# Both softmax attentions one step deeper: values of a head behind turns and scores of the next ones, two buffers of turned copies

## The reference, cut to what matters

```python
# MLA, 8 heads, per block of 128 queries
sc = jnp.einsum('bqhd,bkhd->bhqk', q[:, s:e], k[:, :e]).astype(jnp.float32)
sc = jnp.where(mask[None, None], sc, MASK_VALUE)
p = jax.nn.softmax(sc, axis=-1).astype(v.dtype)
outs.append(jnp.einsum('bhqk,bkhd->bqhd', p, v[:, :e]))
```

## Time and profile before

| | before |
|---|---|
| median of 3 runs | 1555.76 us (1552.83 to 1557.51) |
| profiled execution | 1555.55 us |
| its span | 1553.7 us |
| PE busy | 1458.6 us, 94% |
| DVE busy | 766.3 us, 49% |
| ACT busy | 617.6 us, 40% |
| mean granted clock of PE | 0.942 of full |
| MLA attention | 591 to 661 us of the span |
| MoBA attention | 1135 to 1174 us of the span |

### The profile page before, as it was taken

One profiled execution on the slowest core, in us unless ns is written; L12 is line 12 of the kernel. 1 busy time (PEld: TensorE's weight loads), 2 busy tenths in 40 slices (PEclk: granted clock), 3 DMA queues, 4 the chain that ended last, 5 costly groups with the idle time before them and its releaser, 6 DMA issues.

```text
span 1553.7 us, 26186 instructions
## 1 busy us (share of the span) xinstructions
PE 1458.6 (94%) x10140; PEld 1239.5 (80%) x10140; DVE 766.3 (49%) x1288; ACT 617.6 (40%) x1014; POOL 10.5 (1%) x23
## 2 busy tenths in 40 slices
PE   5999999999998998899999989999878899999996
PEld 4899999899997995489999889799747855555553
DVE  4466654656546663356665456865166431222123
ACT  4445553443434552344444356533143422232222
POOL 0000020000000000000000000000000000000000
PEclk8999999999999997799999989999658899999998
DMA  7654445655555442456555444432003349999992
GB/s 309 127 186 136 136 163 176 231 174 172 173 175 217 161 152 95 155 188 227 190 185 184 161 176 150 138 109 99 23 0 109 109 170 374 370 354 370 370 367 97
DMA packets 80139, 289.65 MB, mean 186 GB/s; under 512 B 9520, under 2 KB 10544, under 8 KB 79920
## 3 DMA queue, kind: packets, MB, share of 16 engines
q1 hardware_dynamic: 77760, 280.00, 50.0%
q0 software_dynamic: 1712, 3.68, 1.5%
q10 hardware_dynamic: 576, 4.65, 0.7%
HBM read 285.14 MB, written 3.15 MB: 186 GB/s over the span
## 4 chain that ended last, share of the span: by engine, by line
PE 84%; DVE 8%; ACT 3%; issue 2%; DMA 2%; SPq 0%; ACTq 0%; DVEq 0%
PE bank L652 17%; PE bank L656 16%; PE bank L655 16%; PE bank L1178 11%; PE bank L1146 4%; DMA ring<-weights 2%; PE bank L716 2%; PE bank L793 2%; PE bank L687 1%; ACT w_hi L1249 1%; PE bank L1168 1%; PE bank L1169 1%; DVE ring_low L1631 1%; DVE sq L1969 1%; PE bank L1008 1%
## 5 line engine op out<-in xcount | busy, mean ns | idle before, releaser
L1631 DVE TENSOR_TENSOR ring_low<-ring,w_hi 128x1024 fp32r<-128x1024 f32 x292 | 356.0, 1224 | 314.5 <-ACT w_hi L1249 311.9
L652 PE MATMUL bank<-hn_hi,w_hi 128*128 128x272 f32 (+1 forms) x1456 | 426.4, 293 | 22.4 <-DVE ring_low L1631 8.6
L656 PE MATMUL bank<-hn_hi,ring_low 128*128 128x272 f32 (+1 forms) x1456 | 419.3, 288 | 0.0
L655 PE MATMUL bank<-hn_low,w_hi 128*128 128x272 f32 (+1 forms) x1456 | 418.7, 288 | 0.0
L1249 ACT ACTIVATE w_hi<-ring 128x1024 fp32r<-128x1024 f32 x292 | 307.3, 1055 | 225.9 <-PE bank L652 181.0
L652 PEld LDWEIGHTS bank<-hn_hi,w_hi 128*128 128x128 f32 x1456 | 278.5, 191 | 29.2 <-DVE hn_low L1650 13.2
L656 PEld LDWEIGHTS bank<-hn_hi,ring_low 128*128 128x128 f32 x1456 | 279.1, 192 | 0.0
L655 PEld LDWEIGHTS bank<-hn_low,w_hi 128*128 128x128 f32 x1456 | 278.7, 191 | 0.2
L652 PE MATMUL bank<-arena_r,w_hi 128*128 128x256 f32 (+1 forms) x848 | 245.4, 289 | 12.0 <-DVE mod L1679 2.9
L656 PE MATMUL bank<-arena_r,ring_low 128*128 128x256 f32 (+1 forms) x848 | 242.9, 286 | 0.0
L655 PE MATMUL bank<-arena_r,w_hi 128*128 128x256 f32 (+1 forms) x848 | 242.4, 286 | 0.0
(11 more groups left out here) (333 smaller groups left out, 1444.1 us busy)
## 6 DMA issues: line engine op xcount, KB each, us to landing
ring<-weights SPq DMA_DIRECT2D x532, 512.0 KB, 4.2
tab<-tables ACTq DMA_DIRECT2D x1, 3129.0 KB, 12.7
skew<-arena POOLq DMA_DIRECT2D x1, 2048.0 KB, 46.5
h<-tokens ACTq DMA_DIRECT2D x2, 544.0 KB, 4.1
tab<-skew POOLq DMA_DIRECT2D x8, 128.0 KB, 3.6
out<-hn SPq DMA_DIRECT2D x8, 128.0 KB, 2.0
tab<-skew POOLq DMA_DIRECT2D x8, 64.0 KB, 3.4
vec<-vectors ACTq DMA_DIRECT2D x1, 321.5 KB, 4.9
```

What stands on the lines that cost most here:

```text
L652: begun = mm(dst[:, 0:cols], wh, high(k), start=k == 0, stop=False)
L655: mm(dst[:, 0:cols], wh, low(k), start=False, stop=False)
L656: last = mm(dst[:, 0:cols], wl, high(k), start=False, stop=k == K - 1)
L1631: tt_(ring_lo[:, slot, :], ring[:, slot, :], w_hi[:, n % SPLITS, :], ALU.subtract).then_inc(S("w_lo_ready"), 1)
```

## The change

The turned buffers pt_m, pt_meta and pt_a get two parts each, by j % 2. For that up_t, which follows pt_a in the arena, moves to a place that is free by then. On TensorE the loop has one round more: round j does T(j), S(j + 2) and then V(j - 1), with M or J of head j - 1 in front. On ACT, store moves from head i - 1 to head i - 2, and ACT makes the meta copy in MLA, which DVE made. On DVE, the function of head i - 1 becomes that of head i - 2, and the last one stands behind the loop. In MLA this function has lost the meta copy and still does low of the head before its own. In MoBA it now does low of its own head, so that low(j) is done in the same round as before and the norm piece one round later.

```diff
-        pt_m = carve(1, 3 * P)
-        pt_meta = carve(1, SEQ)
+        pt_m = carve(2, 3 * P)
+        pt_meta = carve(2, SEQ)
...
-        pt_a = carve(1, 3 * P, at=delta_at + 4 * NP * P)
-        up_t = carve(2, SEQ)
+        pt_a = carve(2, 3 * P, at=delta_at + 4 * NP * P)
+        up_t = carve(2, SEQ, at=2 * DT * SEQ)
...
-            def attention(tag, heads, score, put):
+            def attention(tag, heads, score, turn, put):
...
-                for j in range(heads):
-                    pe.wait_ge(S(tag + "_p"), j + 1)
+                for j in range(heads + 1):
+                    if j < heads:
+                        pe.wait_ge(S(tag + "_p"), j + 1)
+                        if j:
+                            pe.wait_ge(S(tag + "_pt"), j)
+                        turn(j)
+                    scores(j + 2)
                     if j:
-                        pe.wait_ge(S(tag + "_pt"), j)
-                    put(j, lambda: scores(j + 2))
+                        put(j - 1)
...
-            def attention(tag, heads, probs, parts, stat, pt, store):
-                for i in range(heads + 1):
+            def attention(tag, heads, probs, parts, stat, pt, store, ptm=None):
+                for i in range(heads + 2):
...
-                    if i >= 1:
+                    if 1 <= i <= heads:
                         j = i - 1
                         act.wait_ge(S(tag + "_turned"), j + 1)
-                        fn(pt[:, 0, :], bank[6][:, 0:3 * P], ACT.Copy).then_inc(S(tag + "_pt"), 1)
-                        store(j)
+                        fn(pt[:, j % 2, :], bank[6][:, 0:3 * P], ACT.Copy).then_inc(S(tag + "_pt"), 1)
+                        if ptm is not None:
+                            act.wait_ge(S(tag + "_turnedm"), j + 1)
+                            fn(ptm[0:META, j % 2, :], bank[7][0:META, 0:SEQ], ACT.Copy).then_inc(S(tag + "_ptm"), 1)
+                    if i >= 2:
+                        store(i - 2)
...
                         last.then_inc(S(tag + "_p"), 1)
-                        if turned:
-                            turned(j)
+                    if turned and i >= 2:
+                        turned(i - 2)
+                if turned:
+                    turned(heads - 1)
...
             def mla_turned(j):
-                dve.wait_ge(S("mla_turnedm"), j + 1)
-                if j:
-                    dve.wait_ge(tile_done, done(am(j - 1)))
-                nc.vector.tensor_copy(pt_meta[0:META, 0, :], bank[7][0:META, 0:SEQ]).then_inc(S("mla_ptm"), 1)
...
-                if j:
-                    o_a_low(j - 1)
+                o_a_low(j)
...
-            o_a_low(AH - 1)
```

## The result

The changed kernel takes 1568.88 us, the median of five runs (1567.63 to 1571.33), against 1555.76 us before. The ratio is 1.0086, 95% interval 1.0064 to 1.0109. The profiled execution took 1571.33 us, the slowest of the five, with a span of 1569.5 us.

A forecast was written before the change was run, and what follows sets the result against it. MoBA was taken as bound by its loop over scores, DVE's front and p, and the turn, 4.63 us a head. 1555.6 + 13.8 (MoBA) + 3.2 (MLA) = 1572.6, stated as 1572.5; range 1565 to 1577.5, own range 1570.5 to 1574.5.

The forecast's parts named there:

- The loop S, front, p, T: MoBA head: scores, DVE's scale and mask, exponentials times reciprocal sum, turned probabilities; said to set the pace, 4.63 us.
- DVE's low as the new link: MoBA: DVE's subtraction of rounded values waits for the moved values step, delaying the next front; 7.04 us a head against 4.63.
- The tail: MoBA's end, from the turn of head 6 to the last values: 7.9 us against 6.13, +1.8.
- MLA's wait of T(1): MLA: the turn of head 1 directly follows the scores of head 2, so TensorE stands still: +2.3 us.
- the term of 2.2: MLA: turn of head 1 and scores of head 3 come before mod sum 4, at half clock: +2.2 us.
- T(7)'s wait of 1.3: MLA's end: no front follows join 6, so the last turn is ready within the values of head 5: -1.3 us.
- MLA's sum: The whole MLA stage: 2.3 + 2.2 - 1.3 = +3.2 us.
- the clock at the end: MLA's end: last turn, last mod sum and values of head 6 stay at half clock; at full, MLA would be +0.6.
- rival 1: MLA's end: last turn and last mod sum run at full clock, total 1570 us; chance 0.15.
- Rival 2: MLA: clock falls already around join 6, so it and values of head 5 run at half, 2.4 us more, 1575; chance 0.10.
- Rival 3: MLA: one more group of turn, scores and values at half clock, total 1577 to 1579 us; chance 0.06.

The follow-up runs named there:

- run 4: Changed kernel with MoBA's low one head later and scores issued ahead of turns in both attentions, two buffers: 1533.8 us, ratio 0.9856.
- run 8: Changed kernel with MoBA's low one head later and scores issued ahead of turns in MoBA alone: 1549.52 us, ratio 0.9964.
- run 1: Changed kernel with only MoBA's low on DVE put back to one head later: 1553.1 us, ratio 0.9981.
- run 2: Kernel before the change, with only MoBA's low on DVE made that of its own head: 1568.53 us, ratio 1.0079.
- run 6: Changed kernel with scores issued ahead of turns in both attentions, MoBA's low kept at its own head: 1541.58 us, ratio 0.9911.
- run 3: Changed kernel with MoBA's order put back to that of the kernel before, leaving the change in MLA alone: 1554.73 us, ratio 1.0003.
- run 5: Kernel before the change, single buffers kept, with scores issued ahead of turns: 1546.46 us, ratio 0.9935.
- run 7: run 4 with the output layer's first three weight units split one mod sum later inside MLA: 1526.76 us, ratio 0.983.

## Why the prediction was right

**What bounds MoBA: right.** The loop S, front, p, T of 4.63 us was read from rows of one head. Cutting it (runs 4, 8) brought the head to TensorE's and DVE's own work, 3.1 to 4.2 us.

**DVE's low as the new link: right, in place and in size.** Sum over the links: 7.04 us a head. Measured: 7.01, 7.15, 7.14, 7.15, 7.01. T(6) to T(7) was 3.96 for 4.1. The tail as a whole is the weaker part: 7.2 us for 7.9, with V(5) ending 2.2 us after T(6) for 2.5, while the five heads grew by 12.3 for 12.0. So MoBA grew by 13.4 us for 13.8. Run 1 removes the link and the loss, run 2 makes the link alone and the loss, run 6 shortens the way to V and the head shrinks as summed. The signs named ahead for MoBA all came: five T's at 7.0 to 7.15 us behind 3.0 idle us, low waiting 2.97 for ACT, front following at once, clock 0.50.

**MLA's wait of T(1): right.** 2.23 us measured for 2.3; T(1) and S(3) ran at half until M4 (4.9 us, 605.30 to 610.22), as the term of 2.2 had it; T(7)'s wait of 1.3 went.

**MLA's sum: mis-sized.** The term that failed is the clock at the end. I took M7, T(7) and V(6) to be at half as before, +3.2 in all, and held rival 1, +0.6, at 0.15. The stage was to be longer by about 3 us, and it is longer by 0.4 in the changed kernel's profile. In the four traces with MLA as changed (changed kernel, runs 1, 3, 8) MLA takes 69.9, 70.7, 68.3 and 70.3 us, mean 69.8. With MLA as before (before, run 2) it takes 69.5 and 68.6, mean 69.05. The difference of 0.7 is smaller than the spread within the four. M7 took 1.92 us, full clock, in all four and 3.64, half, in the two others. So rival 1 had the outcome right. Its reason is not shown. I argued that the fall follows J6 and not the idle time behind V(5); with the idle time gone and the join kept, the clock stayed, which speaks against me. But run 5 has both, J6 and V(5) and then the same idle 1.26 us ahead of T(6), and M7 still ran at full clock:

```profile
642.44 0.33 PE L887 MATMUL bank<-tab,arena 128*128 128x128 f32 x1 [1.26 <-DVE arena L1856]
...
643.14 1.93 PE L716 MATMUL bank<-ring,small 128*32 128x512 f32 x16
```

So neither the join nor that idle time is enough to bring the clock down, and what does stays open.

**Rival 2, an earlier fall around J6, is refuted.** T(6), J6, V(5) and T(7) stand close together in the changed kernel and ran at 1.00 (651 to 662 above), and J6 took 0.95 us, full clock, in all four traces with MLA as changed. The Trainium skill ("TensorE: Matmul & The Clock Gate", "Part 4: PE-mode transpose") says that transposes don't count as busy in the way matmuls do. That did not make itself felt there: five transposes on either side of the join and V(5) left the clock as it was.

**Rival 3's time** was added up wrongly: MLA +7 with MoBA +13.8 gives 1576.4, not 1577 to 1579. It did not come, so nothing hangs on it.

**The sum.** MoBA +13.4 and MLA +0.7 make 14.1; the medians differ by 13.1. The two profiled spans differ by 15.8. In these profiles the stages between MLA and MoBA, whose program is the same, are 5.3 us longer after. The clock from 692 to 704 us is 0.72 after and 1.00 before, and from 890 to 925 us it is 0.74 and 0.80. Nothing of the change reaches there, so I count it as scatter of the clock, not shown to be more.

Those behind MoBA are 4.2 us shorter. Of this 2.7 us are the sums of the final norm, the same instructions, 6.41 us before and 3.72 after:

```profile
1538.72 6.41 PE L687 MATMUL bank<-sq,ones 128*128 128x256 f32 x16 [3.32 <-ACT sq L1277]
```

```profile
1557.21 3.72 PE L687 MATMUL bank<-sq,ones 128*128 128x256 f32 x16 [3.32 <-ACT sq L1283]
```

Another 1.4 us are the start of the dense layer, and there the prediction had no term. It starts at full clock in the changed kernel and runs 1, 4, 7 and 8, at half in the kernel before and runs 2, 3 and 5, whose MoBA has the old place of V, and in run 6. So this gain seems to come with the new order, where V(6) and V(7) stand together at the end; run 6 has that order too and no such gain, so it is not shown. The moved up buffers are read in the mixture, behind this layer. Runs 1 and 3 have them too and take 1553.1 and 1554.73 us, so their move costs nothing that these runs can tell.

The forecast was 3.6 us too long: 2.5 of it is MLA's sum and 0.4 MoBA's, and the rest is less than the scatter. The measured time lies inside the stated range only because that range took in rival 1.

## What to carry to other kernels

DVE's instructions ran in program order here (front(3) had its scores at 1154.08 and started at 1156.51, behind low(0)), so an instruction that only cleans up (here the low part of a finished head) becomes a link of the critical loop as soon as what it waits for is moved behind the loop's own next step: when a step is moved on one engine, go through every other engine's queue for who reads its result, and for what stands behind that reader. Before buffers are added, ask whether the wait they remove is on the loop: here they were worth 1.8 us of MoBA with the loop uncut and 5.3 with it cut. Cut the loop first, by issuing the next input as soon as its own bank is free, not when a later product of that bank is done.

## What the runs showed of the hardware that I had not expected

The same program part gets a different clock from one execution to the next. MLA up to M4 is identical in the kernel before and in run 2, and M4 took 3.60 us in one and 1.92 in the other, which is this row:

```profile
604.32 1.92 PE L716 MATMUL bank<-ring,small 128*32 128x512 f32 x16
```

The whole stage, with one and the same program, took 68.3 to 70.7 us in four traces. That is larger than MLA's effect of 0.7, so a single profile can't settle such a term.

A stall costs more than its length where it brings the clock down. Run 7 removed an idle time of 4.5 us; the median fell by 7.0 and MLA became 10.3 us shorter in the traces: the stretch behind J5, at 0.50 in run 4, is at 1.00 in run 7. The clock fell at an idle time of 1.26 us ahead of T(6) in the kernel before and in run 2, and did not in run 5, with the same instructions around it. In MoBA TensorE is busy 24.94 of 28 us in run 4, and the clock stays at 0.50 all the same.

Low on DVE and the front behind it start 0.34 us apart for low(0) and low(4) (1156.17 to 1156.51 above) and 0.46 for low(1) to low(3), of which this pair is the first. The shorter ones stand in the heads of 7.01 us, the longer ones in those of 7.14 and 7.15. In run 2 the two take turns: 0.34 for the even heads, 0.45 or 0.46 for the odd ones, with heads of 7.01 and 7.14. What makes the difference stays open; no run varied it:

```profile
1163.17 0.43 DVE L2092 TENSOR_TENSOR arena_r<-bank,arena_r 64x256 fp32r<-64x256 f32 x1 [2.97 <-ACT arena_r L1559]
1163.63 0.56 DVE L2097 SCALAR_TENSOR_TENSOR arena<-bank,tab 128x384 f32<-128x384 f32 x1
```
